# Three expert weight buffer sets in the second layer of a hybrid decoder step

## What is computed

```python
g_sel = jnp.argmax(g_logits, axis=-1)                  # 4 groups of 8 experts
top_v, top_i = lax.top_k(e_in, MOE_TOP_K)              # 2 of the group's 8
combine = jnp.sum(one_hot(eid, 32) * top_w[..., None], axis=1)
for g in range(MOE_GROUPS):
    hg = jnp.einsum('nd,edf->nef', x, w_gate[sl])      # f = 256
    hu = jnp.einsum('nd,edf->nef', x, w_up[sl])
    act = (silu(hg) * hu) * combine[:, sl, None]
    y = y + jnp.einsum('nef,efd->nd', act, w_down[sl])
x = x + y
```

## Time and profile before

| | us |
|---|---|
| median of three runs | 1255.89 |
| lowest and highest | 1254.28, 1257.87 |
| the profiled execution | 1253.5 |
| its span, first to last instruction | 1251.7 |
| TensorE busy | 977.7 (78%) |
| weight loads of TensorE | 598.9 (48%) |
| VectorE busy | 392.8 (31%) |
| GpSimd busy | 336.5 (27%) |
| ScalarE busy | 154.7 (12%) |

### The profile page before, as it was taken

The page is one execution under the profiler, slowest core; times in us unless marked ns, Lnnn a source line. Parts: engine busy times, 40 slices in busy tenths (PEclk is TensorE's granted clock), DMA queues, the critical chain, the costliest instruction groups (busy, mean ns, idle before and its releaser), DMA issues.

```text
span 1251.7 us, 15678 instructions
## 1 busy us (share of the span) xinstructions
PE 977.7 (78%) x5752; PEld 598.9 (48%) x5752; DVE 392.8 (31%) x816; ACT 154.7 (12%) x288; POOL 336.5 (27%) x552
## 2 busy tenths in 40 slices
PE   4999998995388778777955187999928777777777
PEld 3888778443344444444425165444526444443432
DVE  3300154534632222222145950021263221212214
ACT  3210111113100000000122004001140000000012
POOL 0060000486256665666257000000001111111100
PEclk9999899897599999999976587999957999999999
DMA  6126523511679999999553924000046999999982
GB/s 235 47 85 240 195 69 128 179 59 65 238 318 426 423 415 407 392 411 409 206 72 57 127 83 205 0 1 0 1 159 273 423 410 417 397 388 422 408 347 112
DMA packets 53374, 289.32 MB, mean 231 GB/s; under 512 B 11787, under 2 KB 21771, under 8 KB 34599
## 3 DMA queue, kind: packets, MB, share of 16 engines
q1 hardware_dynamic: 38759, 264.71, 54.4%
q0 software_dynamic: 8928, 16.49, 3.5%
q10 hardware_dynamic: 5632, 7.41, 2.7%
HBM read 267.61 MB, written 35.06 MB: 242 GB/s over the span
## 4 chain that ended last, share of the span: by engine, by line
PE 47%; DMA 31%; DVE 8%; POOL 8%; issue 3%; ACT 2%; SPq 1%; DVEq 0%; ACTq 0%; POOLq 0%
DMA arena<-in_w_gu 15%; DMA arena<-in_w_down 14%; PE ps L631 11%; PE ps L949 9%; POOL arena L1779 7%; PE ps L814 6%; PE ps L804 5%; DVE arena L1244 4%; PE ps L850 3%; PE ps L925 2%; PE ps L929 2%; PE ps L856 2%; PE ps L775 1%; PE ps L596 1%; DMA arena<-in_s_d 1%
## 5 line engine op out<-in xcount | busy, mean ns | idle before, releaser
L814 PE MATMUL ps<-arena 128*64 128x256 f32 x2048 | 236.3, 383 | 69.7 <-DMA arena<-in_w_gu 68.2
L814 PEld LDWEIGHTS ps<-arena 128*64 128x64 f32 x2048 | 144.4, 136 | 163.7 <-DMA arena<-in_w_gu 61.7
L804 PE MATMUL ps<-arena 128*64 128x512 f32 x512 | 125.3, 632 | 42.5 <-DMA arena<-in_w_down 41.6
L1851 POOL TENSOR_TENSOR arena<-arena 128x256 f32<-128x256 f32 (+3 forms) x192 | 132.8, 691 | 40.7 <-POOL arena L1851 40.3
L631 PE MATMUL ps<-arena 128*128 128x260 f32 x640 | 142.1, 382 | 0.0
L631 PEld LDWEIGHTS ps<-arena 128*128 128x128 f32 x640 | 120.7, 189 | 19.8 <-issue 0.4
L1779 POOL TENSOR_TENSOR arena<-arena 128x32 f32<-128x32 f32 (+5 forms) x165 | 84.9, 514 | 160.6 <-ACTq L1098 145.2
L949 PE MATMUL ps<-arena 128*128 128x512 f32 x256 | 113.8, 605 | 4.4 <-ACT arena L1216 4.4
L1566 DVE TENSOR_TENSOR arena<-arena,ps 128x128 f32<-128x128 f32 x64 | 18.5, 289 | 282.4 <-ACT arena L1154 282.4
L804 PEld LDWEIGHTS ps<-arena 128*64 128x64 f32 x512 | 42.6, 143 | 104.5 <-issue 104.5
L1244 DVE TENSOR_TENSOR arena<-arena 128x160 f32<-128x160 f32 (+14 forms) x142 | 77.1, 543 | 21.4 <-PE ps L619 7.3
(11 more groups left out here) (219 smaller groups left out, 955.1 us busy)
## 6 DMA issues: line engine op xcount, KB each, us to landing
arena<-in_w_gu SPq DMA_DIRECT2D x64, 2048.0 KB, 12.8
arena<-in_w_down SPq DMA_DIRECT2D x64, 1024.0 KB, 10.4
arena<-in_w_in SPq DMA_DIRECT2D x10, 1024.0 KB, 5.1
scratch_yd<-arena SPq DMA_DIRECT2D x2, 4160.0 KB, 16.0
arena<-scratch_yd SPq DMA_DIRECT2D x16, 512.0 KB, 6.9
arena<-in_w_out SPq DMA_DIRECT2D x1, 4096.0 KB, 12.8
scratch_hd<-arena ACTq DMA_DIRECT2D x8, 512.0 KB
arena<-in_w_glu SPq DMA_DIRECT2D x2, 2048.0 KB, 7.9
```

The source lines that it names most:

```text
L804: mm = pe.matmul(ps[CAP * s:CAP * s + CAP, 6 + b, :], AT[s][:, CAP * f:CAP * f + CAP], WD[s][:, f, 512 * b:512 * b + 512], start=f == 0, s ...
L814: mm = pe.matmul(ps[CAP * f:CAP * f + CAP, 2 + s, 0:256], XT[:, kc, CAP * s:CAP * s + CAP], WGU[s][:, kc, 256 * f:256 * f + 256], start=kc ...
L1851: g_.tensor_tensor(o, x, y, f).then_inc(sem("matrix_steps"), 1)
```

## The change

In layer 2 there are three buffer sets instead of one (`SLOTS = (1, 3)`): pair p uses set p mod 3. The loads of the first three pairs leave `experts(1)` and are issued earlier in SP's queue: pair 0 when the `yT` transposes are done, gate/up of pair 1 when the first GLU half is done, down of pair 1 when the last router logits are done, pair 2 when the normalised rows are stored (`h_out`). The loop on SP then loads pair p+3 where it loaded pair p+1. Down weights, in both layers, are stored and loaded by output columns: one transfer of 1024 KB brings columns 0 to 511 of both experts of a pair, the other columns 512 to 1023. In layer 1 TensorE waits for each half by itself; in layer 2 both halves count on one semaphore. A down buffer is loaded anew when its own half is done.

To make room, the tiles of layer 2's router and experts lie elsewhere (XG, XT, YE, YG, HB, HC and others now have one place for each layer); YE of layer 2 uses the place of the norm weights GB, so that the last norm weights are loaded behind the first two reads of the stored rows, and VectorE waits for them later. TensorE's expert loop of layer 2 is written out for six pairs, run twice, with pairs 12 to 15 behind it.

```diff
+SLOTS = (1, 3)
...
-        WGU = [place(A + 4096 * b, KC, 512) for b in range(2)]
-        WD = [place(A + 8192 + 2048 * b, 2, D) for b in range(2)]
+        WGU = [[[place(A + 4096 * b, KC, 512) for b in range(2)]],
+               [[place(A + at + 4096 * b, KC, 512) for b in range(2)] for at in (8192, 24736, 32928)]]
+        WD = [[[place(A + 8192 + 2048 * b, 4, 512) for b in range(2)]],
+              [[place(A + at + 2048 * b, 4, 512) for b in range(2)] for at in (16384, 20480, 0)]]
...
+            def load_gate_up(l, e, i, s):
+                sp.dma_start(WGU[l][i][s], T["w_gu"][l][bass.ds(e, 1)].rearrange("e p k n -> p (e k) n")
+                             ).then_inc(sem(f"wgu_in_{l}_{i}_{s}"), 16)
+
+            def load_down(l, p, i, b):
+                sp.dma_start(WD[l][i][b], T["w_down"][l][b][bass.ds(p, 1)].rearrange("j p k n -> p (j k) n")
+                             ).then_inc(sem(f"wd_in_{l}_{i if l else b}"), 16)
...
-                        if follows:
-                            for s in range(2):
-                                sp.wait_ge(sem(f"gu_done_{l}"), n + s + 1)
-                                load_gate_up(2 * p + 2 + s, s)
-                            sp.wait_ge(sem(f"down_done_{l}"), n + 2)
-                            for s in range(2):
-                                load_down(2 * p + 2 + s, s)
+                        for s in range(2):
+                            sp.wait_ge(sem(f"gu_done_{l}"), n + s + 1)
+                            load_gate_up(l, 2 * (p + SLOTS[l]) + s, i, s)
+                        for b in range(2):
+                            sp.wait_ge(sem(f"down_done_{l}"), n + b + 1)
+                            load_down(l, p + SLOTS[l], i, b)
...
+                    if l and t == 0:
+                        load(GB, T["norms"][4], "norm_in")
...
-            load(GB, T["norms"][4], "norm_in")
             sp.wait_ge(sem("taps_ready"), 1)
...
             load(WGL[1], T["w_glu"][1], "w_glu_in_2")
-            sp.wait_ge(sem("x_mixed"), 2)
+            ring.wait_full(sp, "yT", KC - 1)
+            for s in range(2):
+                load_gate_up(1, s, 0, s)
+            for b in range(2):
+                load_down(1, 0, 0, b)
+            ring.wait_full(sp, "gl", 0, TILES)
+            for s in range(2):
+                load_gate_up(1, 2 + s, 1, s)
+            sp.wait_ge(sem("stored"), 16 * 11)
+            ring.wait_full(sp, "lg", 1, TILES)
+            for b in range(2):
+                load_down(1, 1, 1, b)
+            sp.wait_ge(sem("h_out"), 160)
+            for s in range(2):
+                load_gate_up(1, 4 + s, 2, s)
+            for b in range(2):
+                load_down(1, 2, 2, b)
             experts(1)
...
-                    def down(p):
-                        for s in range(2):
-                            pe.wait_ge(sem(f"wd_in_{l}_{s}"), 16 * p + 256 * r + 16)
+                    def loads(i):
+                        return -(-(EP - i) // SLOTS[l])
+
+                    def down(p, i, lap):
                         pe.wait_ge(sem(f"at_ready_{l}"), 2 * p + E * r + 2)
                         pe.wait_ge(sem(f"y_ready_{l}"), 2 * p + E * r + 2)
                         for b in range(2):
+                            if l == 0:
+                                pe.wait_ge(sem(f"wd_in_{l}_{b}"), 16 * lap + 256 * r + 16)
+                            elif b == 0:
+                                pe.wait_ge(sem(f"wd_in_{l}_{i}"), 32 * lap + 32 * loads(i) * r + 32)
...
+                        with pe.Fori(0, 2) as k:
+                            for q in range(6):
+                                pair(6 * k + q, q % 2, q % 3, 2 * k + q // 3)
+                        for p in range(12, EP):
+                            pair(p, p % 2, p % 3, p // 3, follows=p < EP - 1)
...
-                        dve.wait_ge(sem("norm_in"), 8 * nn_ + 16)
                         add_last(0)
                         add_last(1)
                         variance(0)
+                        dve.wait_ge(sem("norm_in"), 8 * nn_ + 16)
...
-    down = n["moe_w_down"].reshape(2, E, 2, P, D).transpose(0, 1, 3, 2, 4)
+    down = n["moe_w_down"].reshape(2, EP, 4, P, 2, 512).transpose(0, 4, 1, 3, 2, 5)
```

More of the change, by code:

```diff
@@ new lines, in bass_hybrid_step @@
+        AT = [[place(A + at + P * b, P) for b in range(2)] for at in (15872, 41504)]
+        OHR = [[place(A + 16128 + P * q, P) for q in range(10)],
+               [place(A + 7168 + P * q, P) for q in range(8)] + ACTB[1]]
+        OHT = [place(A + at, 5, P) for at in (16128, 6144)]
+        PICK = [place(A + at, 5, P) for at in (16768, 41760)]
+        YE = [[place(A + 17408 + D * b, D) for b in range(2)], [GB, place(A + 7168, D)]]
+        YL = [place(A + at, 2, 512) for at in (18432, 7168)]
@@ new lines, in bass_hybrid_step @@
+        YG = [[[place(A + at + D * j, D) for j in range(2)] for at in (6144, 4096, 0, 2048)],
+              [[place(A + 24736 + 2048 * t + D * j, D) for j in range(2)] for t in range(4)]]
+        YG[0].append([place(A + at, D) for at in (14336, 17408)])
+        YG[1].append([place(A + at, D) for at in (20480, 22528)])
+        HB = [place(A + at, 5, D) for at in (27872, 32928)]
+        JUNK = [[place(A + at, D) for at in ats] for ats in ((31040, 13312), (41120, 38048))]
+        HTB = [[place(at + 1024 * b, KC, P) for b in range(2)] for at in (A + 25824, A + 20480)]
@@ L515, in turns @@
                         sp.wait_ge(sem(f"h_{2 * l + 2}"), 5)
-                    for s in range(2):
[L517 to L524, removed]
+                    if l == 0 or not isinstance(r, int):
+                        for i in range(SLOTS[l]):
+                            for s in range(2):
+                                load_gate_up(l, 2 * i + s, i, s)
+                            for b in range(2):
+                                load_down(l, i, i, b)
+                    if l == 0:
+                        with sp.Fori(0, EP - 1) as p:
+                            pair(p, 0)
+                    else:
+                        with sp.Fori(0, 4) as k:
+                            for i in range(3):
+                                pair(3 * k + i, i)
+                        pair(12, 0)
                 sp.wait_ge(sem("most_ready"), l + 1)
@@ L539, in experts @@
                             turns(r)
+                    if l:
+                        sp.wait_ge(sem(f"rounds_done_{l}"), 1)
+                        load(GB, T["norms"][4], "norm_in")
                     sp.wait_ge(sem(f"rounds_done_{l}"), 14)
@@ L774, in turns @@
                         for q in range(10):
-                            mm = pe.matmul(ps[:, b, 0:E], OHR[:, q], what[q // 5][:, q % 5], start=q == 0, stop=q == 9)
+                            mm = pe.matmul(ps[:, b, 0:E], OHR[l][q], what[q // 5][:, q % 5], start=q == 0, stop=q == 9)
                         mm.then_inc(sem(f"list_done_{l}"), 1)
@@ L838, in turns @@
                         pe.wait_ge(sem("picks_by_act"), 2 * l + 1)
-                    with pe.Fori(0, E // 4 - 1) as k:
-                        pair(2 * k, 0, True)
-                        pair(2 * k + 1, 1, True)
-                    pair(E // 2 - 2, 0, True)
-                    pair(E // 2 - 1, 1, False)
+                    if l == 0:
+                        with pe.Fori(0, EP // 2 - 1) as k:
+                            for half in range(2):
+                                pair(2 * k + half, half, 0, 2 * k + half)
+                        pair(EP - 2, 0, 0, EP - 2)
+                        pair(EP - 1, 1, 0, EP - 1, follows=False)
+                    else:
+                        with pe.Fori(0, 2) as k:
[3 more added lines that the diff above has]
+                            pair(p, p % 2, p % 3, p // 3, follows=p < EP - 1)
                     if isinstance(r, int):
@@ L1884, in gather @@
                         pool.sem_inc(sem("marks"), 1)
-                        g_.indirect_dma_start(out=XG[half], out_offset=None, in_=hd,
+                        g_.indirect_dma_start(out=XG[l][half], out_offset=None, in_=hd,
                                               in_offset=bass.IndirectOffsetOnAxis(ap=now, axis=0),
```

100 lines of the change are left out of this document (45 added, 55 removed).

## The result

The changed kernel takes 1219.83 us (median of 4 runs, 1215.49 to 1222.25), the kernel before 1256.88 in the same session (4 runs, 1254.28 to 1259.52). The ratio is 0.970, interval 0.967 to 0.973: 37 us less. The forecast was 1221. The profiled execution of after has a time of 1222.25 us, the longest of its four, and a span of 1220.4; that of before had 1253.5 and 1251.7. So the two traces lie 31.3 us apart, not 37, and both are read against each other with that in mind. The loop is 33.6 us shorter in the trace of after (222.5 against 256.1) and 33.3 in that of `again` (222.8); where the last few of the 37 us lie, the traces do not show.

A forecast was written before the change was run, and what follows sets the result against it. The prediction took layer 2's expert loop to be bound by the bytes of its weights. It summed -35 us (loop) and 0 (all else) from 1255.9 to 1221 us, with a range of 1215 to 1233 at about 0.84.

The forecast's parts named there:

- no gain: Rival, layer 2 loop: pace set by something other than bytes, stays 17 us a pair; 1256 us, chance 0.03.
- Part 1, the prefetch: Before layer 2's loop: early loads of pairs 0 to 2 fit into empty DMA time or are hidden; cost 0.
- Part 2, the loop: Layer 2 loop: 13 pairs to load instead of 15, last down matmul 31.4 to 36.1 us earlier; 35 taken.
- The idle part: Layer 2 loop: DMA idle time between 0.9 us at the start only and the old 2.5% share; taken near the low end.
- Part 3, gathers beside a deeper queue: Layer 2 loop: gathers, 3.3 to 14.1 us to landing, fit the 15.2 us available; price 0.
- gathers lag: Rival, layer 2 loop: gathers stand behind the deeper weight queue, TensorE ends a pair later, 12.2 us; 1233 us, chance 0.08.
- Part 4, the split: Down weights by output columns: 0 in layer 2; 0 in layer 1, at most 1.8 us gained there.
- Part 5, the tail: After the last down matmul: norm weights loaded later (1.25 us) stay hidden, the tail keeps its length; 0.
- Part 6, code: TensorE's longer loop code: a fetch at the jump back costs 0 to 14.1 us, covered; sum unchanged.
- slower: Rival, layer 2 loop: TensorE stalls for code in every pair, 21.6 us a pair; 1338 us, chance 0.05.
- the one stall: TensorE's jump back in layer 2's loop: a taken branch stalls once for code, made up over nine later pairs.
- six signs: Profile after: load times, first matmul near 954, no early weight waits, DMA share 0.99, last down matmul near 1179, unchanged tail.

The follow-up runs named there:

- again: The changed kernel run once more, unedited, in a later session: 1220.17 us, ratio 0.970 to the kernel before.
- two_sets: Changed kernel with two buffer sets in layer 2, pair 0 loaded early, pair 1 behind `h_out`: 1238.82 us, ratio 0.986 to the kernel before.
- one_set_early: Changed kernel with one buffer set in layer 2, only pair 0 loaded early, in the GLU stage: 1254.21 us, ratio 0.999 to the kernel before.
- no_gs: Changed kernel with layer 2's gathers from pair 2 on and all its scatters replaced by 1 KB transfers: 1196.56 us, ratio 0.951 to the kernel before.
- even_slots_before: Kernel before the change with two constant tables permuted so an expert's tokens spread over its 64 partitions: 1236.92 us, ratio 0.983.
- late_loads: Changed kernel with three buffer sets, but all first three pairs' loads issued behind `h_out`: 1240.93 us, ratio 0.988 to the kernel before.

## Why the prediction was right, step by step

**What bounds the loop.** Right: bytes. One pair more in the loop cost 14.9 us (`two_sets`), one pair early without a buffer of its own gained nothing (`one_set_early`), and taking 19.6 us of gathers and scatters out shortened it by at least that (`no_gs`). The rival "no gain" is out by the result, and by the first six pairs of after: the round of gather, tokens and scatter runs at 12.0 us a pair when weights are there.

**Part 1, the prefetch.** Right. SyncE's issues in after (start, us, line, transfer):

```profile
773.69 0.81 SPq L499 DMA_DIRECT2D arena<-in_w_gu  x2
774.54 0.94 SPq L503 DMA_DIRECT2D arena<-in_w_down  x2
839.79 0.80 SPq L499 DMA_DIRECT2D arena<-in_w_gu  x2
917.93 0.80 SPq L503 DMA_DIRECT2D arena<-in_w_down  x2
931.32 0.80 SPq L499 DMA_DIRECT2D arena<-in_w_gu  x2
932.16 1.08 SPq L503 DMA_DIRECT2D arena<-in_w_down  x2
958.46 3.76 SPq L499 DMA_DIRECT2D arena<-in_w_gu  x2
```

Forecast: shortly before 777, 839, 917, 929, 958. `h_out` was given 929 and pair 2 went out at 931.32, 2 us late and harmless. The first gate/up matmul started at 954.56 (forecast 953.94, bounds 1 us to each side).

**Part 2, the loop.** The sum held, two of its terms did not.
- The work of q1 was put at 15.35 us a pair, from the loop of before. It is 0.877 x 222.52 = 195.1 us for 13 pairs, 15.0 a pair: mis-sized by 0.35, 4.5 us in all. The row for it was at hand: 6.29 MB at the 418 GB/s of the undisturbed stretch, used in Part 1, are 15.0. The loop of before had moved its bytes at 411 GB/s of q1's busy time (94.64 MB in 230.3 us), that of after at 420 (82.05 in 195.1). The number of sets alone does not make this difference: `even_slots_before`, with one set, has 0.919 x 245.49 / 15 = 15.0 us a pair as well. Its cause stays open.
- The idle part was bounded at 0.9 and 5.6 us (220.0 and 224.7 less 219.1), and 2 taken, because a spare buffer would cover the losses behind slow matmuls. It was 3.5%, 7.8 us, beyond the upper bound. The mechanism named was right: a slow matmul no longer empties the queue (`again`). What failed is the step from there to the whole: the earlier trace rows shows idle time behind one slow matmul, and it was read as all of it, while 3.7 of the 6.4 us lay at the end of the loop already. Some 6 us at the end, of one or two engines that have more rows of gathers and scatters, were in no term and no bound.
- The two errors cancel: 195.1 + 19.6 + 7.8 = 222.5 us, against the 221.1 (256.12 - 35) of the forecast. The last down matmul came at 1180.98, for a forecast of 1179. The total is right by that much luck.
- TensorE's pace: 12.0 us a pair (12.2 forecast). Its first wait for down weights, 0.7 us, comes in pair 7 (1047.94); forecast was about pair 6.

**Part 3, gathers beside a deeper queue.** Right. The gathers of after, against the earlier trace rows:

```profile
DMA to landing us min/median/max: 3.6/9.2/10.5
```

No later with three sets queued than with one, while the weight loads themselves took 46.6 us at most. The rival "gathers lag" is out. This agrees with the rule of the Trainium skill, page "DMA: Bandwidth & Descriptors", section "Queues, rings and completion order", that each DMA engine turns between its queues, which the prediction cites.

**Part 4, the split.** Right in layer 2 (0), open in layer 1 between 0 and 3 us.

**Part 5, the tail.** Right: 34.14 us to VectorE's last instruction in both. The 1.7 us by which the span's end lies later come behind it, and in `again` they are not there.

**Part 6, code.** Right: 6 packets of q8 in the loop instead of 2, and no idle time of TensorE in the six pairs run at its own pace, each 12.0 us; behind the jump back the matmuls of pair 6 start at 1026.82, where the last ones of pair 5 end (1023.22 + 3.61). So neither "slower" nor the one stall happened here.

Of the six signs named, three came as written (loads, first matmul, no weight waits up to pair 5); the last down matmul came 2 us late, the tail kept its length up to VectorE's last instruction; "a DMA share of 0.99 or more from 958 to about 1179" was wrong: 0.96 over the first 18.5 us, and thin for the last 15.

## What to carry to other kernels

Where a loop is bound by bytes, count the bytes that are left when it starts: each set of buffers filled before it takes one turn's load out, and an early load without a buffer of its own takes none. Before calling the rest of such a loop full, look at the DMA share of its last 10 us: 0.5 or 0.06 there says that some engines, or one, have more to do than the others, and in a kernel that gathers rows by index into the first partitions of a tile, spreading the rows costs nothing and gave here 14 us of 1220.

## What the runs showed of the hardware

- Rows moved by index load the DMA engines by partition, as measured above; the time follows the fullest engine in a loop of 200 us, also where most of the bytes are spread evenly. In the loop of before evening them out gained 10.6 us, more than the 6.4 us that its share showed as idle: the idle share went (91.9% and 8.0% are taken by q1 and q0), and q1's own time fell from 230.3 to 225.6 us. Why that fell is not explained. One trace stands on each side, and that of before has three slow matmuls which the other has not.
- With three sets of loads queued, an instruction of SyncE that issues one can take long. The longest of L499 in after took 9.03 us and in `late_loads` 8.98; in `two_sets` it was 0.435, in before (L493) 0.433. Behind them stood only more loads of weights and, after all had been issued, the reads of the stored rows. A load of another kind would have to wait, which no run here shows.
- Two gate/up loads issued as 120 and 8 partitions each (`balance`) brought the rate from about 420 to 221 GB/s with the engines still busy. Why stays open.
